# Split matrix products read and written from the last column to the first, and unread filler products of 240 and 480 columns

## Time and profile before

| | |
|---|---|
| median of 3 runs | 2740.71 us (2739.37, 2740.71, 2748.9) |
| span of the profiled execution | 2752.8 us |
| TensorE (PE) busy | 2686.2 us, 98% of the span, 21,677 products |
| weight loads (PEld) busy | 2605.5 us, 95% |
| VectorE / ScalarE / GpSimd busy | 74% / 55% / 22% |
| mean granted TensorE clock | 0.992 |

### The profile page before, as it was taken

One profiled execution on the slowest core, in us unless ns is written; L12 is line 12 of the kernel. 1 busy time (PEld: TensorE's weight loads), 2 busy tenths in 40 slices (PEclk: granted clock), 3 DMA queues, 4 the chain that ended last, 5 costly groups with the idle time before them and its releaser, 6 DMA issues.

```text
span 2752.8 us, 60778 instructions
## 1 busy us (share of the span) xinstructions
PE 2686.2 (98%) x21677; PEld 2605.5 (95%) x21677; DVE 2041.7 (74%) x4481; ACT 1510.4 (55%) x3283; POOL 606.2 (22%) x647
## 2 busy tenths in 40 slices
PE   9999999999999999999999999999999999999998
PEld 9899989999999999899989999999988999988998
DVE  6769988787887867779888777777668766556655
ACT  6453455555555555652455555555546755556554
POOL 1034780021110204025850010010034300012000
PEclk9999999999999999999999999999999999999999
DMA  5045428787877854156347677676644156542454
GB/s 176 16 150 187 143 69 255 223 295 247 273 264 245 284 169 154 60 174 201 98 142 235 222 241 238 216 246 225 191 131 153 38 157 194 163 153 84 155 184 130
DMA packets 153654, 493.93 MB, mean 179 GB/s; under 512 B 18032, under 2 KB 37936, under 8 KB 153488
## 3 DMA queue, kind: packets, MB, share of 16 engines
q1 hardware_dynamic: 137424, 437.67, 49.1%
q0 software_dynamic: 15488, 54.11, 6.8%
q10 hardware_dynamic: 576, 0.03, 0.0%
HBM read 481.62 MB, written 10.13 MB: 179 GB/s over the span
## 4 chain that ended last, share of the span: by engine, by line
PE 86%; DVE 10%; ACT 2%; issue 1%; POOL 1%; DMA 0%; POOLq 0%; ACTq 0%; DVEq 0%
PE banks L862 68%; PE banks L1106 5%; PE banks L1127 2%; PE banks L1004 2%; DVE meta_row L2419 1%; DVE work L2422 1%; PE banks L900 1%; PE banks L1423 1%; DVE w_lo L553 1%; PE banks L895 1%; PE banks L1270 1%; POOL x_lo L2939 1%; PE banks L1393 1%; ACT w_hi L546 1%; PE banks L1405 1%
## 5 line engine op out<-in xcount | busy, mean ns | idle before, releaser
L553 DVE TENSOR_TENSOR w_lo<-ring,w_hi 128x512 fp32r<-128x512 f32 x1448 | 1015.3, 705 | 517.8 <-ACT w_hi L546 494.8
L546 ACT ACTIVATE w_hi<-ring 128x512 fp32r<-128x512 f32 x1448 | 908.8, 630 | 724.7 <-PE banks L862 704.8
L862 PE MATMUL banks<-gated_all,w_hi 128*128 128x240 f32 (+1 forms) x5120 | 883.6, 276 | 7.2 <-DVE gated_all L2486 7.2
L862 PE MATMUL banks<-x_hi,w_hi 128*128 128x240 f32 (+2 forms) x2752 | 779.8, 283 | 8.4 <-POOL x_lo L2939 6.6
L862 PEld LDWEIGHTS banks<-gated_all,w_hi 128*128 128x128 f32 x5120 | 777.5, 190 | 9.3 <-DVE gated_all L2486 9.3
L862 PE MATMUL banks<-x_hi,w_lo 128*128 128x240 f32 (+2 forms) x2752 | 770.4, 280 | 0.0
L862 PE MATMUL banks<-x_lo,w_hi 128*128 128x240 f32 (+2 forms) x2752 | 765.8, 278 | 0.0
L862 PE MATMUL banks<-gated_all,w_lo 128*128 128x240 f32 (+1 forms) x2560 | 709.7, 277 | 0.0
L862 PEld LDWEIGHTS banks<-x_hi,w_hi 128*128 128x128 f32 x2752 | 525.3, 191 | 19.3 <-POOL x_lo L2939 7.5
L862 PEld LDWEIGHTS banks<-x_lo,w_hi 128*128 128x128 f32 x2752 | 524.4, 191 | 0.4
L862 PEld LDWEIGHTS banks<-x_hi,w_lo 128*128 128x128 f32 x2752 | 522.6, 190 | 0.0
(11 more groups left out here) (388 smaller groups left out, 3215.1 us busy)
## 6 DMA issues: line engine op xcount, KB each, us to landing
ring<-in_peer_v SPq DMA_DIRECT2D x256, 512.0 KB, 3.7
ring<-in_peer_u SPq DMA_DIRECT2D x184, 512.0 KB, 4.5
arena<-in_peer_u SPq DMA_DIRECT2D x72, 512.0 KB, 3.7
ring<-in_mlp_up SPq DMA_DIRECT2D x64, 512.0 KB, 3.5
ring<-in_mlp_down SPq DMA_DIRECT2D x64, 512.0 KB, 3.5
ring<-w_peer_query SPq DMA_DIRECT2D x32, 512.0 KB, 3.5
ring<-w_fox_proj SPq DMA_DIRECT2D x24, 512.0 KB, 3.6
ring<-w_nsa_proj SPq DMA_DIRECT2D x20, 512.0 KB, 3.5
```

What stands on the lines that cost most here:

```text
L546: act.activation(w_hi[:, hn % SPLITS], raw_half(hn), ACT.Copy).then_inc(hi_ready, 1)
L553: dve.tensor_tensor(w_lo[:, hn % SPLITS], raw_half(hn), w_hi[:, hn % SPLITS].bitcast(F32), ALU.subtract)\
L862: mm = pe.matmul(out, w_at(w), x, start=start and j == 0, stop=stop and j == 2, skip_group_check=True)
```

## The change

In `three`, both the output bank's columns and the moving operand's columns are given in reverse: column 239 (or 255, or 271) is read and written first, column 0 last. Each result still lands in the same place. The stationary operand, the order of the products and the waits are as before.

In `keep_warm`, WARM_DIFF goes from 20 to 14, and a call whose `n` equals WARM_DIFF now alternates a product of 240 columns (`gated_hi`, first half) with one of 480 (first halves of `gated_hi` and `gated_lo`), both read straight. WARM_SCALE is 14 too, so every call with WARM_SCALE takes this branch as well. WARM_LOAD is 20, which equalled WARM_DIFF before and does not now: its 20 products read straight instead of permuted.

```diff
-WARM_DIFF, WARM_FILL = 20, 6
+WARM_DIFF, WARM_FILL = 14, 6
...
             def three(out, w_at, xh, xl, start, stop):
 
                 for j, (w, x) in enumerate(((w_hi, xh), (w_hi, xl), (w_lo, xh))):
-                    mm = pe.matmul(out, w_at(w), x, start=start and j == 0, stop=stop and j == 2, skip_group_check=True)
+                    mm = pe.matmul(out[:, ::-1], w_at(w), x[:, ::-1], start=start and j == 0, stop=stop and j == 2,
+                                   skip_group_check=True)
                 return mm
...
                 if n in (WARM_SCALE, WARM_DIFF):
                     parts, at = next(by_scale, (2, 48))
                     src = in_lines(at, parts)
-                for _ in range(n):
-                    pe.matmul(banks[:, bank, 0:SEQ], gated_all[:, 0:P], src, start=True, stop=True)
+                for k in range(n):
+                    if n == WARM_DIFF and k % 2:
+                        pe.matmul(banks[:, bank, 0:2 * MOVED], gated_all[:, 0:P], gated_both[:, :, 0, 0:MOVED], start=True, stop=True)
+                    else:
+                        pe.matmul(banks[:, bank, 0:MOVED if n == WARM_DIFF else SEQ], gated_all[:, 0:P],
+                                  gated_both[:, 0, 0, 0:MOVED] if n == WARM_DIFF else src, start=True, stop=True)
```

## The result

The changed kernel took 2763.51 us (median of 4 runs, 2757.32 to 2765.81) beside 2741.09 us of the kernel before (4 runs, 2739.37 to 2748.9): a ratio of 1.0069, 95% interval 1.0048 to 1.0090. Slower, then, and by a little more than the 0.5% that the prediction set as its bound. The profiled execution of the changed kernel has a span of 2759.8 us and a time of 2761.63 us.

The account below looks back on a forecast made before the run. The prediction took TensorE's split products on line 862, paced by weight loads, to bound the kernel. 2740.7 us + 0 for the reversal + 2.5 for the filler = 2743 us; range 2670 to 2830 us.

Parts of the forecast that it names:

- the forecast case: Whole kernel: pace of the split products stays the same, 2727 to 2754 us; chance 0.36.
- the rival of a worse state: Split products settle at slower paces, 256 columns at 120 ns: 54 us more, 2797 us; chance 0.20.
- What bounds the kernel: Line 862's split products set the time, 68% of the chain; weight loads put a floor of 109 to 112 ns.
- The reversal at zero: Split products on line 862: reading and writing columns in reverse costs zero, 256-column paces staying about midway.
- The floor for gains: Split products with only the weight load left gain up to 45 us; faster rival at 2698 us, chance 0.25.
- Half rate: Descending columns of split products move at half rate: 1,589 us more, 4332 us; chance 0.19.
- the worry about the write: PSUM writes at column step -1 might count as not contiguous; taken strictly, time near the worst end, 1,589 us more.
- The filler: Six keep_warm calls of 14 grow by 0.6 us each, partly in idle time: 0 to 2.6 us, taken as 2.5.

Follow-up runs that it names:

- filler: Kernel before with only the edit of the filler calls, split products still read and written straight: 2749.03 us beside 2751.93 us, ratio 0.9996.
- write: Kernel before with only the output bank written from last column to first, moving operand read ascending: 2749.47 us, ratio 0.9986.
- 240 alone: Kernel before with the split products' read and write reversed only at 240 columns: 2748.15 us beside 2752.13 us, ratio 0.9993.
- the two with unread streams: Kernel before, its 20 unread products ahead of differential attention replaced by blocks of 45 varying width, direction and start: spans 2935.9 and 2969.9 us.
- reversal: Kernel before with split products' read and write both reversed, filler calls unchanged: 2765.77 us beside 2751.93 us, ratio 1.0057.
- read: Kernel before with only the moving operand read from last column to first, bank written ascending: 2764.28 us beside 2751.93 us, ratio 1.0046.
- 256 alone: Kernel before with the split products' read and write reversed only at 256 columns: 2757.00 us beside 2747.73 us, ratio 1.0029.

## Why the prediction came out as it did

The forecast was 2743 us with no measurable change as the likeliest case; measured were 2763.51 us. That is above the 2727 to 2754 us of the forecast case. It is inside the range because the range takes in the rival of a worse state, which had a chance of 0.20 and came true at its near end.

**What bounds the kernel** held: line 862 on the chain with 69%, no new wait, and a floor near 112 ns under the 240-column products. The floor of "109 to 112 ns" can be read more closely: without the first, which came early, the products of 48 columns are 111.6 ns apart too. That it is the weight load that makes this floor fits these rows, but no run took it away.

**The reversal at zero** is the step that failed: for the 256-column products above all, and for those of 272 columns by a little. For 240 columns it held: with these 10,560 products alone reversed the ratio is 0.9993 (0.9970 to 1.0017). Only their share was a slip: 10,560 of 16,896 products are 62.5% in number, and not 70%, which is the share of all split products in the span; no term of the sum hangs on it. For 256 columns the prediction took a mix of states that stays about midway. The states are real, but the direction of the read decides which of them can be had. Ten profiled kernels read from the old start. In six of them (before, filler, write, 240 alone and the two with unread streams) the MLP stages read in ascending order, and seven of these twelve stages stood at 113.5 ns; in the other four (changed, reversal, read, 256 alone) they read in descending order, and none of the eight did. In numbers: the ascending cases average (7 x 113.5 + 5 x 118.0) / 12 = 115.4 ns, so the descending 118.0 cost 2.6 x 4,992 = 13 us. The 272s add 1.4 x 1,344 = 2 us. Together 15 us or 0.5%, an estimate that agrees with 1.0057 and lies inside the interval of the first result. Beside the 256s alone, whose interval ends at 13 us, it is at the upper end.

**The floor for gains** was right in kind: no stretch of a dense stage got under 112.0 ns, and the gain of up to 45 us did not come. The reason that the prediction gave for a gain, that the two paces show how the moving read and the weight load disturb each other, is not in the rows: they show that there are two paces, and not why.

**The rival of a worse state** is the one that came true, at a smaller size than priced: 256 columns at 118.0 in the MLP stages and not 120 (+2.6 instead of +4.3 ns; of the shorter streams that of 192 products shown above is at 120.0), 272 at 125.0 and not 128.2, and 240 unmoved instead of +2.6 ns. Its 54 us shrink to 15. Its mark (both MLP stages at 118 to 120 ns) is what the profile shows; the other half of its condition, 240s that lose 0.3 ns, did not come.

**Half rate** fell wholly, and with it the worry about the write: 0.9986 for the write alone. The Trainium skill, Advanced Engine Details and Errata, section SBUF Cachelines, asks for two hits on a line of 16 bytes and says nothing of direction; a descending fp32 read has four hits a line and still lost the pace of 113.5 ns at 256 columns. By that rule the time would not have changed; the measurement decides.

**The filler** held: 2.39 us a call for 14 products at the full clock, the wait behind it eaten, and a ratio of 0.9996.

What stays open: why a descending read has no good pace at 256 columns. That the moving read and the weight load get in each other's way was argued, but no run took the weight load away or turned it round. Nor was it shown what draws the pace of an ascending stream in a real stage; the unread streams only show that the way in has a part in it. That the drawn paces make the 25 us spread of the kernel before is an estimate: 1.4 ns by 10,560 and 4.5 ns by 4,992 give up to 37 us between all bad and all good.

## What to carry to other kernels

A stream of products can have several stable paces for one shape. Read the pace from long pieces of the chain, in several executions, before putting a difference down to an edit. Sort products by width: here those at the floor (240 columns) did not feel how their operand is read, while those a little wider (256 and 272) did. And when an edit turns two things round at once, run each alone; here the write was free and the read was not.

## What was not expected of the hardware

- At the start that the real streams use, the long streams keep to a few paces. The same values, 112.0 or 113.3 ns for 240 columns and 113.3, 117.8 or 120.0 ns for 256, came back in other kernels, other stages and unread streams. At other starts there are values between them, such as 116.7 and 118.3 ns.
- At 256 columns the direction of the read matters, and that of the write does not: no descending read was under 117.7 ns, ascending ones reach 113.3.
- At 256 columns the start of the moving operand matters in steps of 16 bytes: ascending, 113.3 or 117.8 ns at start 0, 119 ns at start 4 and 120.0 ns at start 16.
- At 512 columns the direction makes no difference: 233.6 and 233.5 ns. At 384 it makes one of 1.3 ns, 174.7 and 176.0.
